# A state-space mixer on one core: convolution kernels stored in eight shifted copies, each Toeplitz block read by one 128-partition transfer

## The chip, the cores and the metric

The program runs on one core of a Trainium2 chip. TensorE (PE) multiplies, VectorE (DVE), ScalarE (ACT) and GpSimd (POOL) work elementwise, and SyncE (SP) issues transfers. ACT issues transfers too, in line with its own instructions. The metric is the device time of one execution in microseconds; the number quoted is the median of the runs.

## The reference

Sixteen meta tokens and 512 frames of width 1024, 528 positions in all, go through two layers. Layer 0 mixes along time with a diagonal state-space model; layer 1 is a windowed attention. Each layer ends with a gated feed-forward block with a short causal convolution. What matters here is the mixer of layer 0, which works on 64 groups of 16 channels, each with 64 complex states:

```python
bu = jnp.einsum('blgh,gph->blgp', ug, b_bar)
_, states = lax.associative_scan(_ssm_combine, (a, bu), axis=1)
y = jnp.einsum('blgp,ghp->blgh', states, c).real.reshape(bsz, seq_len, D_MODEL)
y = y + d_skip.astype(f32) * u32
g = jax.nn.gelu(y).astype(u.dtype)
val, gate = jnp.split(g @ w_glu, 2, axis=-1)
return val * jax.nn.sigmoid(gate)
```

## The kernel before

The mixer cuts the 528 positions into 66 chunks of T = 8 steps. Inside a chunk the recurrence is a block Toeplitz matrix (one 128 by 128 matrix for each group: 8 steps of 16 channels in, 8 steps of 16 channels out). Between chunks a scan carries the state. The 64 groups go in eight blocks of eight.

For block `b` the steps are these:

- `in_map(b)` on DVE (block 7: `input_maps` on POOL) builds the map from inputs to states, `win_t`, from powers of lambda (`own[0]`, in PSUM) and `bbar`. `input_map(b)` on PE transposes it, and on ACT it copies it to `win`.
- The normalized input `xn` is written by ACT at L783, eight instructions, one for each time step. `inputs(b)` on PE transposes it group by group, and `input_copy` on ACT copies it to `u5`, whose 128 rows are (time step, channel).
- `kernels(b)` on PE makes the convolution kernel of lags 0 to 7, and ACT copies it (L722) behind 112 columns of zeros into `kern`, 240 columns wide; the rows are (group, channel in).
- `kernel_out(b)` on ACT's queue stores those 240 columns to DRAM (`kern_scratch`).
- `kernel_in(b)` on SP's queue waits for that store and reads the Toeplitz block back into `toep` with `kernel_rows`: for each input time step t the window of 128 columns that starts at (7 - t)*16, to the 16 partitions of that step, so eight transfers for a block.
- `additions(b)` on PE and `states(b)` on DVE make the chunk states. `outputs(b)`, on PE, adds the Toeplitz product (L1179) and the states' part (L1185). Its results are called y0 to y7 below.
- `gelu(b)` on ACT evicts y, `gelu_out(b)` stores it to DRAM, and `gelu_in(b)` reads it back in eight transfers (four issued by SP, four by ACT) with channels on partitions. `glu_operand(b)` splits it for the following product `w_glu` (the GLU, L1266).

Each engine's order is written out by hand. y6 and y7 use the same two PSUM banks, so `outputs(7)` may begin only when `gelu(6)` has evicted y6; it also waits for `toep_in[7]` and for `states(7)` (`z_ready`). `toep` holds four blocks, so `kernel_in(7)` waits for y3. SP's order in this stretch is: `gelu_in(b - 4)`, then `kernel_in(b)`, for b from 4 to 7. On ACT, `kernels(b)` waits for the store of block b - 2, since `kern` has two buffers.

After the mixer PE runs the GLU, the feed-forward blocks and the attention, nearly all of it at one line, L1266.

Of the kernel before, what the change touches and what calls it, by code (L numbers as in the profile page):

```python
# [27 lines left out]
F32 = mybir.dt.float32  # L28
F32R = mybir.dt.float32r
I32 = mybir.dt.int32  # L30
ACT = mybir.ActivationFunctionType
# [3 lines left out]
P = 128  # L35
D = 1024
SEQ = 512
META = 16
L = SEQ + META
# [7 lines left out]
T = 8  # L47
# [94 lines left out]
def trunk(nc, x, meta, s5_norm, s5_lambda_re, s5_lambda_im, s5_log_step, s5_b_re, s5_b_im, s5_c_re, s5_c_im,  # L142
# [90 lines left out]
    ltmp = [at(f"ltmp{n}", Z_ZST + 512 * n, 512) for n in range(2)]  # L233
    junk = at("junk", Z_B, 2 * D)
    Z_TOEP = Z_B + G * NC + 2 * PAIRS * (T + 1) * HC
    xn = at("xn", Z_TOEP, G * TH)[:].rearrange("p (g t h) -> p g t h", g=G, t=T)
    xt_meta = at("xt_meta", Z_B + G * NC + PAIRS * (T + 1) * HC, D)

    zc = Zone(Z_C, C_COLS)
# [29 lines left out]

    zh = Zone(Z_H, KD * L)  # L270
    rhot = zh.put("rhot", PAIRS * NV)[:].rearrange("p (q c) -> p q c", q=PAIRS)
    win_t = at("win_t", Z_H + 4 * L, 2 * 2 * 4 * TH)[:].rearrange("p (b r q t h) -> p b r q t h", b=2, r=2, q=4, t=T)

    gy = x_raw.rearrange("p k (n x c) -> p k n x c", n=4, x=2)
    zh = Zone(Z_H, KD * L)
# [8 lines left out]
    same = at("same", pads(Z_SPL)[0] + 2 * TH - HC, HC)  # L284
    skip = at("skip", pads(Z_RAW)[0], KD * HC)[:].rearrange("p (k h) -> p k h", k=KD)

    kern_scratch = nc.dram_tensor("kern_scratch", (8, 8, HC, 2 * TH - HC), F32, kind="Internal").ap()
    gelu_scratch = nc.dram_tensor("gelu_scratch", (8, P, 8, NC), F32, kind="Internal").ap()

    craw = [at(f"craw{r}", Z_SPL + W_AT[r] * P, KD * S)[:].rearrange("p (e s) -> p e s", e=KD) for r in range(2)]  # L290
# [52 lines left out]
    with ctx:  # L343
# [104 lines left out]
        def bank_gone(eng, name):  # L448
# [5 lines left out]
            else:  # L454
                eng.wait_ge(gy_ready, n + 1)

        def kernel_rows(eng, b):

            for t in range(T):
                src = kern_scratch[b].rearrange("g h c -> h g c")  # L460
                eng.dma_start(toep[t * HC:(t + 1) * HC, 8 * (b % 4):8 * (b % 4 + 1), :],  # L461
                              src[:, :, (T - 1 - t) * HC:(2 * T - 1 - t) * HC]).then_inc(toep_in[b], 16)

        def gelu_rows(eng, k, groups):

# [164 lines left out]
        def _(act):  # L630
# [26 lines left out]

            def kernel_out(b):
                act.wait_ge(kern_ready, b + 1)
                act.dma_start(kern_scratch[b].rearrange("g h c -> (g h) c"), kern[b % 2][:, :]  # L660
                              ).then_inc(kern_out[b % 2], 16)

            act.dma_start(g5row[0:2, :].rearrange("p (q h) -> p q h", h=HC),
                          s5_norm[0].rearrange("(q t h) -> t q h", t=2, h=HC)).then_inc(g5_in, 16)
# [115 lines left out]
            conv_rows()  # L780
            act.wait_ge(rst5_ready, 1)
            for t in range(T):
                run(xn[0:NC, :, t, :], xc[0:NC, t * D:(t + 1) * D].rearrange("c (g h) -> c g h", g=G), ACT.Copy,  # L783
                    scale=rst5[0:NC, t:t + 1]).then_inc(xn_ready, 1)
            act.wait_ge(xn_ready, T)
            input_map(0)
# [282 lines left out]
        def _(pe):  # L1069
# [43 lines left out]
            def inputs(b):  # L1113
                if b == 0:
                    pe.wait_ge(xn_ready, T)

                    pe.wait_ge(bbar_ready, 1)
                pe.wait_ge(first_copied, U_COPIED + b - 2 if b >= 2 else C_COPIED)
                for n in range(8):
                    ins = tr(slot[b % 2][:, n // 4, (n % 4) * NC:(n % 4 + 1) * NC],  # L1120
                             xn[0:NC, 8 * b + n].rearrange("c t h -> c (t h)"), ident[0:NC, 0:NC])
                ins.then_inc(first_full, 1)

            def input_map(b):

                pe.wait_ge(*((win_dve, b + 1) if b < POOL_MAPS else (win_pool, b + 1 - POOL_MAPS)))
                if b == 0:
                    pe.wait_ge(first_copied, CONV_COPIED)
                for r in range(2):
                    ps = begin_bank(f"w{b}{'ab'[r]}")  # L1130
                    for q in range(4):
                        ins = tr(ps[:, q * P:(q + 1) * P], win_t[:, b % 2, r, q].rearrange("p t h -> p (t h)"),
                                 ident[:, :])
                    ins.then_inc(bank_full, 1)

# [31 lines left out]

            def outputs(k):

                pe.wait_ge(toep_in[k], 16 * T)  # L1170
                pe.wait_ge(z_ready, k + 1)
                ps = [begin_bank(f"y{k}{x}") for x in "ab"]

                for n in range(4):
                    o = lambda x, rows: ps[x][rows, n * NC:(n + 1) * NC]
                    for x in range(2):
                        g = 8 * k + 2 * n + x
                        for rows in (slice(0, S), slice(S, P)):
# [406 lines left out]
        def _(dve):  # L1585
# [124 lines left out]
            def in_map(b):  # L1710

                if b >= 2:
                    bank_wait(dve, f"w{b - 2}b")
                lp = [own[0][:, r * T * PAIRS:(r + 1) * T * PAIRS].rearrange("p (k q) -> p k q", k=T)
                      [:, T - 1::-1, 4 * b:4 * b + 4].rearrange("p t q -> p q t")[:, :, :, None]
                      .to_broadcast([P, 4, T, HC]) for r in range(2)]
                bb = [bbar[r][:, 4 * b:4 * b + 4, None, :].to_broadcast([P, 4, T, HC]) for r in range(2)]
                tmp = own[1].rearrange("p (q t h) -> p q t h", q=4, t=T)
                o = [win_t[:, b % 2, r] for r in range(2)]
                tt(o[0], lp[0], bb[0], ALU.mult)  # L1720
                tt(o[1], lp[0], bb[1], ALU.mult)
                link(tt(tmp, lp[1], bb[1], ALU.mult))
                link(tt(o[0], o[0], tmp, ALU.subtract))
                link(tt(tmp, lp[1], bb[0], ALU.mult))  # L1724
                tt(o[1], o[1], tmp, ALU.add).then_inc(win_dve, 1)
                dve.wait_ge(win_dve, b + 1)
# [260 lines left out]
        def _(pool):  # L1987
# [50 lines left out]
            def input_maps(b):  # L2038

                bank_wait(pool, f"w{b - 2}b")  # L2040
                lp = [lpow[r][:, T - 1::-1, 4 * b:4 * b + 4].rearrange("p t q -> p q t")[:, :, :, None]
                      .to_broadcast([P, 4, T, HC]) for r in range(2)]
                bb = [bbar[r][:, 4 * b:4 * b + 4, None, :].to_broadcast([P, 4, T, HC]) for r in range(2)]
                o = [win_t[:, b % 2, r] for r in range(2)]
                tmp = ptmp[:, :].rearrange("p (q t h) -> p q t h", q=4, t=T)
                tt(o[0], lp[0], bb[0], ALU.mult)
                link(tt(tmp, lp[1], bb[1], ALU.mult))
                tt(o[1], lp[0], bb[1], ALU.mult)
                link(tt(o[0], o[0], tmp, ALU.subtract))
                link(tt(tmp, lp[1], bb[0], ALU.mult))  # L2050
                tt(o[1], o[1], tmp, ALU.add).then_inc(win_pool, 1)
                pool.wait_ge(win_pool, b + 1 - POOL_MAPS)
# [182 lines left out]
```

## Time and profile before

| | |
|---|---|
| runs | 1170.57, 1170.91, 1167.56 us; median 1170.57 |
| profiled execution, first to last instruction (span) | 1166.7 us |
| PE busy | 1111.7 us (95% of the span) |
| DVE, ACT, POOL busy | 501.5, 484.8, 628.7 us |
| `toep` transfers | 64 of 64 KB, median 2.9 us from issue to landing |
| `kern_scratch` stores | 8 of 120 KB, median 2.8 us to landing |
| `gelu_scratch` stores | 8 of 264 KB, median 3.1 us to landing |

The page gives the profiled execution's span and no separate total; the span lies 0.9 us below the fastest run and 3.9 us below the median. The chain of waits follows the last instruction back through what released it, so its pieces add up to the span. A timeline row gives the start, the duration, the engine, the line, and in brackets how long the engine had been idle and what ended that. Rows of SPq and ACTq are those queues' issues of transfers, not the transfers themselves.

### The profile page before, as it was taken

To read this page: it belongs to the slowest core of one execution; us is meant where nothing else is said; L and a number is where in the kernel's file an instruction comes from. 1 tells how busy PE (TensorE), PEld (TensorE's weight loads), DVE (VectorE), ACT (ScalarE), POOL (GpSimd) and SP (SyncE) were. 2 spreads that over 40 slices of the span, in tenths; PEclk is the share of its full clock that TensorE was granted. 3 is DMA by queue.
4 is the path that set the end of the run, shared out by engine and by line. 5 is a ranking of instruction groups with operands and counts; after the bars stand their busy time and mean duration, and the time that the engine had idled before them with its cause. 6 is when DMAs were issued, how large, how long until landed. Compare 5 with 4: busy or idle time off the path is not lost.

```text
span 1166.7 us, 27411 instructions
## 1 busy us (share of the span) xinstructions
PE 1111.7 (95%) x10092; PEld 1070.7 (92%) x10092; DVE 501.5 (43%) x862; ACT 484.8 (42%) x885; POOL 628.7 (54%) x533
## 2 busy tenths in 40 slices
PE   4577999999999999999999999999999999999997
PEld 3466999999999999999999999999999999988887
DVE  8898312354444444211115777435444444430111
ACT  4843333354444444322324545445444444432222
POOL 4991255455555555654544454765555555565551
PEclk7598899999999999999999999999999999999999
DMA  7168432233333333333323333323333333333321
GB/s 153 31 180 177 96 94 86 74 104 88 88 88 89 89 90 94 108 92 88 96 63 84 94 102 83 88 76 102 93 93 91 90 90 90 99 110 92 95 73 73
DMA packets 221973, 110.50 MB, mean 95 GB/s; under 512 B 33271, under 2 KB 219527, under 8 KB 221591
## 3 DMA queue, kind: packets, MB, share of 16 engines
q1 hardware_dynamic: 214823, 105.41, 33.0%
q10 hardware_dynamic: 7090, 4.26, 1.4%
q8 instruction: 41, 0.67, 0.2%
q14 instruction: 19, 0.16, 0.0%
HBM read 103.31 MB, written 6.32 MB: 94 GB/s over the span
## 4 chain that ended last, share of the span: by engine, by line
PE 91%; DVE 5%; ACT 2%; issue 1%; DMA 0%; SPq 0%; POOL 0%; ACTq 0%; DVEq 0%
PE slot L1266 81%; PE slot L1547 1%; PE slot L1411 1%; PE slot L1185 1%; PE slot L1179 1%; PE slot L1462 1%; ACT xn L783 1%; PE slot L1463 1%; PE slot L1441 1%; PE slot L1148 1%; PE slot L1204 0%; DMA toep<-kern_scratch 0%; SPq L461 0%; PE slot L1524 0%; DVE slot L1724 0%
## 5 line engine op out<-in xcount | busy, mean ns | idle before, releaser
L2065 POOL TENSOR_TENSOR w_lo<-raw,w_hi 128x512 fp32r<-128x512 f32 (+2 forms) x312 | 430.6, 1383 | 428.0 <-ACT w_hi L638 409.9
L638 ACT ACTIVATE w_hi<-raw 128x512 fp32r<-128x512 f32 (+2 forms) x308 | 202.9, 662 | 394.8 <-PE slot L1266 384.5
L1266 PE MATMUL slot<-xa_hi,w_hi 128*128 128x264 f32 (+1 forms) x1472 | 298.7, 284 | 0.9 <-DVE xa_lo L1808 0.9
L1266 PE MATMUL slot<-xa_hi,w_lo 128*128 128x264 f32 (+1 forms) x1472 | 298.5, 284 | 0.0
L1266 PE MATMUL slot<-xa_lo,w_hi 128*128 128x264 f32 (+1 forms) x1472 | 298.3, 284 | 0.0
L1266 PEld LDWEIGHTS slot<-xa_hi,w_hi 128*128 128x128 f32 x1472 | 229.0, 189 | 1.3 <-issue 1.1
L1266 PEld LDWEIGHTS slot<-xa_lo,w_hi 128*128 128x128 f32 x1472 | 228.3, 189 | 0.0
L1266 PEld LDWEIGHTS slot<-xa_hi,w_lo 128*128 128x128 f32 x1472 | 227.8, 189 | 0.0
L1837 DVE TENSOR_TENSOR slot<-slot,rinv 128x528 f32<-128x528 f32 (+1 forms) x88 | 62.5, 710 | 166.8 <-PE slot L1266 166.5
L1266 PE MATMUL slot<-act_hi,w_hi 128*128 128x264 f32 (+1 forms) x506 | 132.1, 318 | 0.0
L1266 PE MATMUL slot<-act_hi,w_lo 128*128 128x264 f32 (+1 forms) x506 | 132.0, 317 | 0.0
L1266 PE MATMUL slot<-act_lo,w_hi 128*128 128x264 f32 (+1 forms) x506 | 131.7, 317 | 0.0
L1783 DVE TENSOR_TENSOR h<-slot,h 128x528 f32 (+5 forms) x23 | 16.1, 698 | 205.6 <-PE slot L1266 205.6
L1840 DVE SCALAR_TENSOR_TENSOR cbuf<-slot,conv_w,cbuf 128x528 f32<-128x528 f32 (+1 forms) x88 | 66.8, 759 | 86.3 <-ACT cbuf L900 86.3
L1266 PEld LDWEIGHTS slot<-act_lo,w_hi 128*128 128x128 f32 x506 | 83.4, 188 | 6.6
L1266 PEld LDWEIGHTS slot<-act_hi,w_lo 128*128 128x128 f32 x506 | 83.2, 188 | 6.6
L1266 PEld LDWEIGHTS slot<-act_hi,w_hi 128*128 128x128 f32 x506 | 83.4, 188 | 6.3
L1842 DVE SCALAR_TENSOR_TENSOR cbuf<-slot,conv_w,cbuf 128x528 f32<-128x528 f32 (+1 forms) x88 | 66.8, 759 | 11.5 <-DVE cbuf L1840 1.7
L900 ACT ACTIVATE cbuf<-slot,conv_w 128x528 f32<-128x528 f32 (+1 forms) x88 | 61.1, 694 | 22.7 <-DVE slot L1837 22.3
L2112 POOL TENSOR_TENSOR act_lo<-abuf,act_hi 128x528 f32 (+3 forms) x44 | 57.7, 1312 | 17.3 <-ACT act_hi L909 17.3
L905 ACT ACTIVATE slot<-cbuf 128x528 f32<-128x528 f32 (+1 forms) x44 | 26.8, 609 | 77.3 <-DVE cbuf L1842 77.3
L1266 PE MATMUL slot<-xg_hi,w_hi 128*128 128x264 f32 x256 | 53.4, 290 | 0.0
(298 smaller groups left out, 1542.9 us busy)
## 6 DMA issues: line engine op xcount, KB each, us to landing
raw<-in_ffn_w_up SPq DMA_DIRECT2D x176, 256.0 KB, 2.9
raw<-in_ffn_w_down SPq DMA_DIRECT2D x32, 384.0 KB, 3.4
raw<-in_ffn_w_down SPq DMA_DIRECT2D x32, 320.0 KB, 3.0
raw<-in_s_w_glu SPq DMA_DIRECT2D x32, 256.0 KB, 2.8
toep<-kern_scratch SPq DMA_DIRECT2D x64, 64.0 KB, 2.9
raw<-in_w_q SPq DMA_DIRECT2D x16, 256.0 KB, 3.2
raw<-in_w_o SPq DMA_DIRECT2D x16, 256.0 KB, 3.0
gelu_scratch<-x_raw ACTq DMA_DIRECT2D x8, 264.0 KB, 3.1
```

The costliest lines, as they stand in the source:

```text
L638: run(buffer_of(w_hi_all, buf, nk), buffer_of(raw_all, buf, nk), ACT.Copy).then_inc(hi_done, 1)
L783: run(xn[0:NC, :, t, :], xc[0:NC, t * D:(t + 1) * D].rearrange("c (g h) -> c g h", g=G), ACT.Copy, scale=rst5[0:NC, t:t + 1]).then_inc(xn_ ...
L900: run(cbuf[:, q, real:L], ubuf_of(q)[:, 2 + real:L + 2], ACT.Copy, scale=w).then_inc(tap_done[p], 1)
L905: run(ubuf_of(0)[:, 2 + real:L + 2], cbuf[:, 0, real:L], ACT.Silu).then_inc(silu_done[p], 1)
L1148: ins = mm(flat(b % 2)[t * S:(t + 1) * S, col:col + NV], win[b][:, r, q, t * S:(t + 1) * S], u5[:, 2 * (4 * b + q) + t, 0:NV], start=True, ...
L1266: ins = mm(slot[dst][:, half, 0:b - a], w, xx[:, k, a:b], start=k == 0 and n == 0, stop=k == nk - 1 and n == 2)
L1783: tt(hm, product(e), hm, ALU.add).then_inc(h_done[p], 1)
L1837: tt(halves(ubuf_of(q)[:, 2 + live:L + 2]), (acc_of, live_of)[l](q), halves(rinv[:, live:L]), ALU.mult).then_inc(up_evicted[p], 1)
L1840: link(stt(cbuf[:, q, real:L], ubuf_of(q)[:, 1 + real:L + 1], w(q, 1), cbuf[:, q, real:L], ALU.mult, ALU.add))
L1842: ins = stt(cbuf[:, q, real:L], ubuf_of(q)[:, real:L], w(q, 0), cbuf[:, q, real:L], ALU.mult, ALU.add)
L2065: tt(buffer_of(w_lo_all, buf, nk), buffer_of(raw_all, buf, nk), f32(buffer_of(w_hi_all, buf, nk)), ALU.subtract).then_inc(lo_done, 1)
L2112: tt(tile_of(act_lo, m, real), abuf[:, real:L], f32(tile_of(act_hi, m, real)), ALU.subtract).then_inc(act_lo_done[p], 1)
```

## The change

`kern_scratch` now holds for each block and each (group, channel in) row eight windows of 128 columns, shifted by 16 columns each, instead of the 240 columns once: the store writes 512 KB in rows of 512 bytes, from overlapping parts of `kern`, not 120 KB in rows of 960 bytes. `toep` is then read by one transfer on 128 partitions, 512 KB, not by eight on 16 partitions of 64 KB. The rows of `toep` are now ordered (channel, reversed time step), not (time step, channel). `u5`, and before it `xn` and `win_t`, have the same order: ACT writes `xn` at every eighth column, and `in_map` and `input_maps` run through time in the innermost place and through the channel outside it, with the powers of lambda in rising order.

```diff
-    xn = at("xn", Z_TOEP, G * TH)[:].rearrange("p (g t h) -> p g t h", g=G, t=T)
+    xn = at("xn", Z_TOEP, G * TH)[:].rearrange("p (g h t) -> p g h t", g=G, t=T)
...
-    kern_scratch = nc.dram_tensor("kern_scratch", (8, 8, HC, 2 * TH - HC), F32, kind="Internal").ap()
+    kern_scratch = nc.dram_tensor("kern_scratch", (8, P, T, TH), F32, kind="Internal").ap()
...
+        def windows(t):
+
+            a = t[:, 0:TH]
+            return bass.AP(tensor=a.tensor, offset=a.offset, ap=[a.ap[0], [HC, T], [1, TH]])
+
         def kernel_rows(eng, b):
 
-            for t in range(T):
-                src = kern_scratch[b].rearrange("g h c -> h g c")
-                eng.dma_start(toep[t * HC:(t + 1) * HC, 8 * (b % 4):8 * (b % 4 + 1), :],
-                              src[:, :, (T - 1 - t) * HC:(2 * T - 1 - t) * HC]).then_inc(toep_in[b], 16)
+            eng.dma_start(toep[:, 8 * (b % 4):8 * (b % 4 + 1), :],
+                          kern_scratch[b].rearrange("(g h) t c -> (h t) g c", h=HC)).then_inc(toep_in[b], 16)
...
-                act.dma_start(kern_scratch[b].rearrange("g h c -> (g h) c"), kern[b % 2][:, :]
-                              ).then_inc(kern_out[b % 2], 16)
+                act.dma_start(kern_scratch[b], windows(kern[b % 2])).then_inc(kern_out[b % 2], 16)
...
-                run(xn[0:NC, :, t, :], xc[0:NC, t * D:(t + 1) * D].rearrange("c (g h) -> c g h", g=G), ACT.Copy,
+                run(xn[0:NC, :, :, T - 1 - t], xc[0:NC, t * D:(t + 1) * D].rearrange("c (g h) -> c g h", g=G), ACT.Copy,
...
-                pe.wait_ge(toep_in[k], 16 * T)
+                pe.wait_ge(toep_in[k], 16)
...
-                      [:, T - 1::-1, 4 * b:4 * b + 4].rearrange("p t q -> p q t")[:, :, :, None]
-                      .to_broadcast([P, 4, T, HC]) for r in range(2)]
-                bb = [bbar[r][:, 4 * b:4 * b + 4, None, :].to_broadcast([P, 4, T, HC]) for r in range(2)]
+                      [:, :, 4 * b:4 * b + 4].rearrange("p t q -> p q t")[:, :, None, :]
+                      .to_broadcast([P, 4, HC, T]) for r in range(2)]
+                bb = [bbar[r][:, 4 * b:4 * b + 4, :, None].to_broadcast([P, 4, HC, T]) for r in range(2)]
```

SP's queue from `kernel_in(0)` to `gelu_in(4)`, before (`toep` is the Toeplitz block, `xt` the input for the residual stream, `x_raw` the GELU result read back):

```order
L461 DMA toep<-kern_scratch 16x8x128 x8
L522 DMA xt<-in_x 128x4x128 x8
L461 DMA toep<-kern_scratch 16x8x128 x24
L467 DMA x_raw<-gelu_scratch 16x8x66 x4
L461 DMA toep<-kern_scratch 16x8x128 x8
L467 DMA x_raw<-gelu_scratch 16x8x66 x4
L461 DMA toep<-kern_scratch 16x8x128 x8
L467 DMA x_raw<-gelu_scratch 16x8x66 x4
L461 DMA toep<-kern_scratch 16x8x128 x8
L467 DMA x_raw<-gelu_scratch 16x8x66 x4
L461 DMA toep<-kern_scratch 16x8x128 x8
L538 DMA xt_meta<-in_meta 16x1024
```

The same place with the change:

```order
L464 DMA toep<-kern_scratch 128x8x128
L525 DMA xt<-in_x 128x4x128 x8
L464 DMA toep<-kern_scratch 128x8x128 x3
L470 DMA x_raw<-gelu_scratch 16x8x66 x4
L464 DMA toep<-kern_scratch 128x8x128
L470 DMA x_raw<-gelu_scratch 16x8x66 x4
L464 DMA toep<-kern_scratch 128x8x128
L470 DMA x_raw<-gelu_scratch 16x8x66 x4
L464 DMA toep<-kern_scratch 128x8x128
L470 DMA x_raw<-gelu_scratch 16x8x66 x4
L464 DMA toep<-kern_scratch 128x8x128
L541 DMA xt_meta<-in_meta 16x1024
```

Each block has one issue in the place of eight; the sequence of steps is the same. On ACT the order stays as it was, and only the store's form differs; its rows of the change around the stores of blocks 1 to 3 are:

```order
L724 ACTIVATE kern_135<-slot 128x128
L663 DMA kern_scratch<-kern_135 1024x1x128
L715 ACTIVATE win_73<-slot 128x512 x2
L724 ACTIVATE kern_134<-slot 128x128
L663 DMA kern_scratch<-kern_134 1024x1x128
L715 ACTIVATE win_74<-slot 128x512 x2
L724 ACTIVATE kern_135<-slot 128x128
L663 DMA kern_scratch<-kern_135 1024x1x128
L752 ACTIVATE rhot<-rho 128x24x64
```

Before, those stores read `kern_scratch<-kern 128x240`; nothing else moved.

## Rows read from the trace of the kernel before

**Rows 1.** Chain of waits around y7: start us, length us, what.
```profile
109.44 3.97 DMA toep<-kern_scratch
...
113.46 0.71 PE slot L1179 x8
...
118.68 9.42 PE slot L1266 x60
```

**Rows 2.** Timeline of PE: y5 first and last, y6 first, y7 first.
```profile
102.14 0.45 PE L1179 MATMUL slot<-u,toep 128*64 128x66 f32 x8
...
104.86 0.46 PE L1185 MATMUL slot<-zst,cpow 64*64 64x66 f32 x16
107.80 0.45 PE L1179 MATMUL slot<-u,toep 128*64 128x66 f32 x8 [2.48 <-DMA toep<-kern_scratch]
...
113.46 0.71 PE L1179 MATMUL slot<-u,toep 128*64 128x66 f32 x8 [1.37 <-DMA toep<-kern_scratch]
```

**Rows 3.** Timeline of SP's queue: the eight issues of block 7.
```profile
105.23 4.65 SPq L461 DMA_DIRECT2D toep<-kern_scratch  x8
```

**Rows 4.** Timeline of DVE: the last instruction of states(0) and of states(7).
```profile
70.18 0.70 DVE L1753 TENSOR_TENSOR zst<-zprod,slot 128x520 f32<-128x520 f32 x1
...
109.30 0.70 DVE L1753 TENSOR_TENSOR zst<-zprod,slot 128x520 f32<-128x520 f32 x1
```

**Rows 5.** Timeline of ACT: kernel 3 evicted, store of block 7, gelu(5).
```profile
67.71 0.28 ACT L722 ACTIVATE kern<-slot 128x128 f32<-128x128 f32 x1 [0.48 <-PE slot L1165]
...
97.72 0.37 ACTq L660 DMA_DIRECT2D kern_scratch<-kern  x1
...
105.48 0.61 ACT L756 ACTIVATE x_raw<-slot 128x528 f32<-128x528 f32 x1 [0.36 <-PE slot L1185]
```

**Rows 6.** Windows: stretch, busy of five engines, then PEclk, DMA share, GB/s.
```profile
113.40:118.60 5.20, 5.14 (x96) 4.16 (x96) 0.71 (x1) 0.64 (x1) 0.00 (x0) 0.50 1.07 232
118.60:122.70 4.10, 4.10 (x22) 4.09 (x19) 0.15 (x1) 1.26 (x2) 0.00 (x0) 0.50 1.08 236
122.70:128.00 5.30, 5.30 (x44) 5.18 (x42) 1.27 (x2) 0.65 (x1) 0.00 (x0) 0.99 0.31 56
```

**Rows 7.** Timeline of PE: a shorter idle time earlier in the mixer.
```profile
65.44 1.09 PE L1132 MATMUL slot<-ident,win_t 128*128 128x128 f32 x8 [1.54 <-DVE win_t L1725]
```

**Rows 8.** DMA from 48 to 56 us (queue: packets, MB, share; then issues).
```profile
q1 hardware_dynamic: 1138, 0.52, 29.0%
q10 hardware_dynamic: 144, 0.12, 4.5%
...
toep<-kern_scratch SPq DMA_DIRECT2D x8, 64.0 KB, 2.4
kern_scratch<-kern ACTq DMA_DIRECT2D x1, 120.0 KB, 1.7
```

**Rows 9.** DMA from 77 to 113 us, the same view.
```profile
q1 hardware_dynamic: 8297, 3.23, 51.2%
q10 hardware_dynamic: 4320, 2.79, 29.9%
```

**Rows 10.** Groups by line on ACT: count, busy us, mean ns, idle before.
```profile
L783 ACT ACTIVATE xn<-xc,rst 66x1024 f32<-66x1024 f32 x8 | 8.4, 1135 | 1.6 <-DVE rst L1700 1.6
```

**Rows 11.** Groups by line on DVE, the same columns.
```profile
L1815 DVE TENSOR_TENSOR h<-h,sig 128x528 f32 x6 | 7.0, 1160 | 0.9 <-DVE sig L1813 0.5
...
L1813 DVE TENSOR_TENSOR sig<-slot,sig 128x528 f32<-128x528 f32 x8 | 5.7, 708 | 63.8 <-ACT sig L871 63.8
...
L1697 DVE TENSOR_TENSOR bbar<-cg,slot 128x512 f32<-128x512 f32 x1 | 0.7, 681 | 0.0
...
L1630 DVE MEMSET lpow<- 128x32 f32 x2 | 0.1, 85 | 0.1
...
L1673 DVE MEMSET phase<- 128x32 f32 x1 | 0.1, 85 | 0.0
```

**Rows 12.** Timeline of POOL: the end of its part in the mixer.
```profile
85.51 1.28 POOL L2035 TENSOR_TENSOR cpow<-cpow,ptmp 128x512 f32<-128x512 f32 x1
```

More of the change, by code:

```diff
@@ L271, in trunk @@
     rhot = zh.put("rhot", PAIRS * NV)[:].rearrange("p (q c) -> p q c", q=PAIRS)
-    win_t = at("win_t", Z_H + 4 * L, 2 * 2 * 4 * TH)[:].rearrange("p (b r q t h) -> p b r q t h", b=2, r=2, q=4, t=T)
+    win_t = at("win_t", Z_H + 4 * L, 2 * 2 * 4 * TH)[:].rearrange("p (b r q h t) -> p b r q h t", b=2, r=2, q=4, t=T)
     gy = x_raw.rearrange("p k (n x c) -> p k n x c", n=4, x=2)
@@ L1120, in inputs @@
                     ins = tr(slot[b % 2][:, n // 4, (n % 4) * NC:(n % 4 + 1) * NC],
-                             xn[0:NC, 8 * b + n].rearrange("c t h -> c (t h)"), ident[0:NC, 0:NC])
+                             xn[0:NC, 8 * b + n].rearrange("c h t -> c (h t)"), ident[0:NC, 0:NC])
                 ins.then_inc(first_full, 1)
@@ L1131, in input_map @@
                     for q in range(4):
-                        ins = tr(ps[:, q * P:(q + 1) * P], win_t[:, b % 2, r, q].rearrange("p t h -> p (t h)"),
+                        ins = tr(ps[:, q * P:(q + 1) * P], win_t[:, b % 2, r, q].rearrange("p h t -> p (h t)"),
                                  ident[:, :])
@@ L1714, in in_map @@
                 lp = [own[0][:, r * T * PAIRS:(r + 1) * T * PAIRS].rearrange("p (k q) -> p k q", k=T)
-                      [:, T - 1::-1, 4 * b:4 * b + 4].rearrange("p t q -> p q t")[:, :, :, None]
-                      .to_broadcast([P, 4, T, HC]) for r in range(2)]
-                bb = [bbar[r][:, 4 * b:4 * b + 4, None, :].to_broadcast([P, 4, T, HC]) for r in range(2)]
-                tmp = own[1].rearrange("p (q t h) -> p q t h", q=4, t=T)
+                      [:, :, 4 * b:4 * b + 4].rearrange("p t q -> p q t")[:, :, None, :]
+                      .to_broadcast([P, 4, HC, T]) for r in range(2)]
+                bb = [bbar[r][:, 4 * b:4 * b + 4, :, None].to_broadcast([P, 4, HC, T]) for r in range(2)]
+                tmp = own[1].rearrange("p (q h t) -> p q h t", q=4, t=T)
                 o = [win_t[:, b % 2, r] for r in range(2)]
@@ L2040, in input_maps @@
                 bank_wait(pool, f"w{b - 2}b")
-                lp = [lpow[r][:, T - 1::-1, 4 * b:4 * b + 4].rearrange("p t q -> p q t")[:, :, :, None]
-                      .to_broadcast([P, 4, T, HC]) for r in range(2)]
-                bb = [bbar[r][:, 4 * b:4 * b + 4, None, :].to_broadcast([P, 4, T, HC]) for r in range(2)]
+                lp = [lpow[r][:, 0:T, 4 * b:4 * b + 4].rearrange("p t q -> p q t")[:, :, None, :]
+                      .to_broadcast([P, 4, HC, T]) for r in range(2)]
+                bb = [bbar[r][:, 4 * b:4 * b + 4, :, None].to_broadcast([P, 4, HC, T]) for r in range(2)]
                 o = [win_t[:, b % 2, r] for r in range(2)]
-                tmp = ptmp[:, :].rearrange("p (q t h) -> p q t h", q=4, t=T)
+                tmp = ptmp[:, :].rearrange("p (q h t) -> p q h t", q=4, t=T)
                 tt(o[0], lp[0], bb[0], ALU.mult)
```

## The prediction

> **What bounds the kernel now.** The page's busy times (the table above) come first: PE works 1111.7 of 1166.7 us, so a change off PE pays only where PE stands still or runs slowly. The chain of waits tells where that is near the change. Most of the mixer hangs on DVE and PE in turn; at its end the transfer of the last Toeplitz block stands alone for 3.97 us, then come y7 and the GLU [rows 1]. PE's timeline shows the same transfer twice: y6 starts 2.48 us late, y7 1.37 us late, both released by `toep` [rows 2]. It was late because SP needed 4.65 us for eight issues from 105.23 on, and only the last one's landing counts [rows 3, 1], though the store it reads had been issued at 97.72 [rows 5].
>
> The windows show what these waits cost beyond themselves. PE's granted clock is 0.50, the 1.2 GHz level, in y7 and in the first 4.1 us of the GLU, and 0.99, the 2.4 GHz level, after that [rows 6]. y7 takes 118.68 - 113.46 = 5.22 us [rows 1]; y5, at full clock, takes 102.14 to 105.32, 3.18 us [rows 2].
>
> **The change, part by part.**
>
> *Issues on SP.* One issue takes the place of eight. At 4.65/8 = 0.58 us each [rows 3] seven fewer save 4.1 us on SP for every block. A block read whole has no late last part: it counts from its only issue.
>
> *The read.* Alone on the queues, 1138 packets (nearly all 512-byte rows of `toep`) took 29.0% of 16 engines over 8 us: 37.1 us, or 32.6 ns each [rows 8]. A block is 1024 such rows in either form, 1024 x 32.6 / 16 = 2.1 us of all engines. An eighth of it, 0.26 us, lands after 2.4 us [rows 8], so 2.1 us are fixed; the whole lands after about 4.2 us alone. Between 77 and 113 us the two queues keep the engines 81% busy [rows 9], so I take 5 us (ends: 4.2, and double that).
>
> *The store.* It had 128 rows; queue 10's 144 packets of 960 bytes took 4.5%, 5.8 us, 40 ns each [rows 8], or 0.3 us of all engines, and it landed after 1.7 us. Now 1024 rows at 32.6 ns are 2.1 us: 1.8 us more, so about 3.5 us alone; in traffic I take 5. The four stores in the stretch add 7.1 us to its 29.2 us of transfers (81% of 36 us) [rows 9]. This is the change's own cost, and it lies in the same queues that it relieves. Its issue on ACT took 0.37 us [rows 5]; SP's 0.58 bounds it from above, and 0.2 us once on the path (store 6) is all that adds.
>
> *When y6 and y7 can start.* Block 7: store issued at 97.72, landed at 102.7, read issued at once (SP's wait for y3 is then over), landed at about 108.3. Block 6 is a step of the mixer earlier and easily in time. So neither transfer ends the wait, and what is late next does. y6 needs the banks of y5: gelu(5) runs 105.48 to 106.09 [rows 5], and with 0.2 us to hand over (0.16 from y5's end to gelu(5)) y6 starts at 106.3 and, at 3.18 us, ends at 109.5. gelu(6) then takes 0.2 + 0.61 us, to 110.3. states(7) ends at 110.0 [rows 4]. So y7 starts at 110.5 and not at 113.46: **3.0 us** gained.
>
> *The clock.* PE would stand still for 1.0 us twice, in the place of 2.48 and 1.37 us. Earlier it stood still for 1.54 us and went on at full rate, eight transposes in 1.09 us [rows 7]. I take it that the clock stays up: y7 in 3.18, not 5.22 us, **2.0 us**; the GLU's first 4.10 us at 0.50 in 4.10 x 0.50 / 0.99 = 2.07 us [rows 6], **2.0 us**. The GLU's later operands hang on gelu(7), which moves with y7.
>
> *`xn`.* ACT writes it in eight instructions on the path, 8.4 us [rows 10]. They now write every eighth column, 32 bytes apart. No row shows ACT doing that. The ends: DVE's memset of 32 columns at far distances takes 85 ns, like the one on adjacent columns [rows 11], so nothing; and DVE's sum with one operand read at a stride takes 1160 ns where the product without takes 708 [rows 11], 0.45 us for 528 elements, 0.86 ns each, so 8 x 1024 x 0.86 = 7.0 us. I take nothing, since the memset is the row of a strided write, but it is too short to be sure.
>
> The Trainium skill, SBUF — State Buffer (section Door 1: the DMA port swizzle), says that SBUF has 16-byte lines and that each access that crosses to a new line pays a penalty, without its size. By that every element of the new `xn` write would pay; the sum would then hold the 7.0 us above and come to about zero. The strided read agrees with it; the memset does not.
>
> *`in_map`.* Only the powers of lambda are now read at a stride, 128 bytes apart in PSUM. The product at L1697 reads PSUM in just that way and takes 681 ns for 512 elements, no more than 708 for 528 without [rows 11]: nothing. On POOL block 7's four products read strided SBUF; if each took double (1.1 us more), POOL would end 4.4 us later than 86.8 [rows 12], at 91.2, still 6.5 us before the store of block 7, whose kernel needs it [rows 5]. PE's transposes and products read whole rows as before: nothing.
>
> *ACT's wait for stores.* Kernel 3 may be evicted only when the store of block 1 has landed; at 67.71 it had waited for PE alone [rows 5]. That store falls into the input's transfers, and its 1.8 us more of work (double it for the traffic) may push the eviction by up to 3.6 us. y0 and its banks wait for states(0), which end at 70.9 [rows 4], 2.9 us after the eviction, and for PE's additions behind them: covered, but for 0.7 us at the worst.
>
> **Sum**: 3.0 + 2.0 + 2.0 = 7.0 us. On the profiled span 1166.7 becomes 1159.7. That span lies 3.9 us below the median of the runs, and I set the 7.0 against the median: 1170.57 - 7.0 = **1163.6 us**. About 0.3%, 3.5 us, can be told from no change.
>
> **Rivals.**
>
> *Crowded transfers, or the clock stays down.* If stores and reads, with 7.1 us more of traffic in the same queues, land late by some 2 to 3 us, y7 starts near 112, and the long wait keeps the clock low: 1.5 us gained. If y7 starts at 110.5 but the clock falls as it did, 3.0 us. With the clock back half way, 4 to 5. For it: queues at 81%. Against it: 2.2 us of slack before y7. Together 1166 to 1169, say 1167.3.
>
> *`xn` at the strided price.* +7.0 - 7.0: **1170.5**, no change. Were the clock gain missed too, 1174.5. By itself this makes the kernel slower than before from 0.86 ns for an element on (7.0 us over 8192), and measurably from 1.28 ns: a write at a third of the rate (8.4 us become 25) would give 1180. For it: the strided read; against it: the memset. It shows in one row.
>
> *The change does not do what it says.* The single read could land as late as the last of the eight did, at 113.4 (109.44 + 3.97) [rows 1], if the engines were saturated. Then y7 stays at 113.4: 1170.6. The 4.2 us worked out above speaks against it.
>
> **How the numbers follow.** Chances: forecast 0.45; crowded transfers or low clock 0.22; strided `xn` 0.25 (of which slower than measurable 0.12); no effect, or the stores hold ACT up, 0.08. The predicted time is the likeliest, 1163.6. That case with the runs' own scatter spans 1161.5 to 1165.5; the range reaches over the second case and the even end of the third, **1161.5 to 1174**, and leaves out the steep `xn` cases above and a larger gain below. Faster by more than 0.3%: 0.45 + half of the second, 0.11 = 0.56. Slower: 0.12 + 0.03 = 0.15. The rest, 0.29, is no change.
>
> **What would show it.** Eight `toep` issues, landing 4 to 6 us; stores landing 3.5 to 6; y6 and y7 released by ACT or DVE, no longer by `toep`; granted clock 0.9 or more in y7 and the GLU's start; the eight `xn` instructions at 8.4 us. The forecast is wrong if `xn` takes 12 us or more, if `toep` still stands in the chain before y7, or if the clock is 0.50 there still.

## The result and the profile after: slower by half a per cent

The changed kernel took 1174.80 us (median of 5 runs, 1171.25 to 1175.53), beside 1168.70 us for the kernel before (5 runs, 1166.86 to 1170.91). The ratio is 1.0048, 95% interval 1.0034 to 1.0063: **5.6 us slower** (0.0048 x 1168.70), between 4.0 and 7.4. The forecast was 1163.6, and 1174.80 lies 0.8 us above its range. The forecast took its 7.0 us off 1170.57, the median of the first three of these five runs; by all five the kernel before stands 1.9 us lower. The profiled execution has a span of 1172.8 us, 6.1 more than before.

First the groups by line on ACT, the answer to [rows 10] (busy us, mean ns of one, idle before):

```profile
L785 ACT ACTIVATE xn<-xc,rst 66x1024 f32<-66x1024 f32 x8 | 15.5, 2128 | 1.1 <-DVE rst L1702 1.1
```

Eight instructions take 15.5 us where they took 8.4: **7.1 us more**, all on the path. The timelines of PE and DVE show who waits (start us, length us, engine, line, operation, and in brackets the idle time before and what ended it):

```profile
47.24 2.02 PE L1122 MATMUL slot<-ident,xn 66*128 66x66 f32 x16 [7.32 <-ACT xn L785]
```
```profile
55.71 0.69 DVE L1722 TENSOR_TENSOR win_t<-slot,bbar 128x512 f32<-128x512 f32 x1 [9.61 <-PE slot L1134]
...
116.00 0.70 DVE L1755 TENSOR_TENSOR zst<-zprod,slot 128x520 f32<-128x520 f32 x1
```

PE stands still for 7.32 us for `xn`, and DVE stands still for 9.61 us because of that. The last instruction of states(7) starts at 116.00, 6.7 us later than before (109.30 [rows 4]). That delay never shrinks on the way: the last instruction of states(0) comes at 76.89, 6.7 us later too (70.18 [rows 4]), and y7, which ACT releases in the end, starts 6.8 us later (120.24, before 113.46 [rows 2]).

Then the transfers, from 77 to 113 us as in [rows 9] (queue: packets, MB, share; then issues: KB each, median us to landing):

```profile
q10 hardware_dynamic: 7639, 4.36, 40.2%
q1 hardware_dynamic: 8123, 3.47, 36.4%
...
toep<-kern_scratch SPq DMA_DIRECT2D x5, 512.0 KB, 4.5
kern_scratch<-kern ACTq DMA_DIRECT2D x4, 512.0 KB, 6.1
```

One issue for a block, landing after 4.5 us, and stores landing after 6.1: much as forecast (5 and 5). The share of ACT's queue went from 29.9 to 40.2%. PE's timeline is the answer to [rows 2]:

```profile
96.86 0.45 PE L1150 MATMUL slot<-u,win 128*64 128x65 f32 x6 [1.36 <-issue]
...
110.89 0.45 PE L1181 MATMUL slot<-u,toep 128*64 128x66 f32 x8 [0.77 <-ACT x_raw L758]
...
115.30 0.46 PE L1181 MATMUL slot<-u,toep 128*64 128x66 f32 x8 [1.02 <-ACT x_raw L758]
...
120.24 0.45 PE L1181 MATMUL slot<-u,toep 128*64 128x66 f32 x8 [1.62 <-ACT x_raw L758]
```

`toep` releases nothing any more, so this part of the change does what it says. In its place stand waits for ACT's GELU before y5, y6 and y7, and a standstill of 1.36 us in the middle of the additions before y3, ended by nothing that the profile shows ("issue"). ACT's timeline shows why it is late for the GELU:

```profile
91.14 0.52 ACTq L663 DMA_DIRECT2D kern_scratch<-kern  x1
91.70 4.21 ACTq L470 DMA_DIRECT2D x_raw<-gelu_scratch  x4
...
115.51 3.24 ACTq L470 DMA_DIRECT2D x_raw<-gelu_scratch  x4
118.85 0.64 ACT L766 ACTIVATE xg_hi<-x_raw 128x528 fp32r<-128x528 f32 x1 [3.80 <-issue]
119.40 0.59 ACT L758 ACTIVATE x_raw<-slot 128x528 f32<-128x528 f32 x1
```

The four issues that read GELU rows back take 4.21 us behind a store of 1024 rows, and gelu(6), at 119.40, stands in the same instruction stream behind four such issues and an operand copy. Last the windows, as [rows 6] (the column before the last two is the granted clock):

```profile
118.00:122.00 4.00, 2.38 (x72) 1.97 (x70) 0.72 (x2) 1.14 (x2) 0.00 (x0) 0.97 0.98 237
122.00:128.00 6.00, 6.00 (x64) 5.50 (x63) 0.71 (x1) 1.63 (x3) 0.00 (x0) 0.50 0.96 225
```

PE is at the 2.4 GHz level (granted clock 0.97) until 122 and at 1.2 GHz (0.50) for the rest of y7 and the GLU's start. y7 takes 124.44 - 120.24 = 4.20 us in place of 5.22, and that 1.0 us is all the clock gave.

### The profile page after: what moved, and what is told of

Read it like the earlier page. It is cut to its first block, busy times and chain, and to the rows that moved or that the text cites. A ratio compares the mean times of both kernels' runs of the same rounds, so it can differ in the third digit from the quotient of the medians.

```text
span 1172.8 us, 27355 instructions
## 1 busy us (share of the span) xinstructions
PE 1109.1 (95%) x10092; PEld 1068.6 (91%) x10092; DVE 500.9 (43%) x862; ACT 491.8 (42%) x885; POOL 629.7 (54%) x533
## 4 chain that ended last, share of the span: by engine, by line
PE 90%; DVE 5%; ACT 3%; issue 1%; DMA 1%; ACTq 1%; SPq 0%; DVEq 0%
PE slot L1268 81%; PE slot L1549 1%; ACT xn L785 1%; PE slot L1413 1%; PE slot L1464 1%; PE slot L1187 1%; PE slot L1181 1%; PE slot L1465 1%; PE slot L1443 1%; ACTq L470 1%; PE slot L1150 0%; PE slot L1206 0%; DMA v_scratch<-vtok 0%; PE slot L1526 0%; DVE slot L1726 0%
```

## The experiments

Three parts had to be told apart: the strided write of `xn`, the larger store, and the single read. Each of the first runs undoes some of them or does some of them alone; later ones change the order of the issues or the engine that writes. Times are ratios to the kernel before on the same chip, with the 95% interval; us are the ratio's difference from 1 times some 1169 us.

**The change with `xn` in runs of 16.**
```diff
-    xn = ... .rearrange("p (g h t) -> p g h t", g=G, t=T)
+    xn = ... .rearrange("p (g t h) -> p g t h", g=G, t=T)
-                run(xn[0:NC, :, :, T - 1 - t], ...
+                run(xn[0:NC, :, T - 1 - t, :], ...
```


> Leaves out the right order of the rows of xn: the changed kernel, but ACT writes xn in runs of 16 channels of one time step again and the transposes take the rows as they lie, so the values fed to the mixer are in another order than the powers expect. All else as in the changed kernel: stores in eight copies, one read for a block, POOL's and DVE's products at a stride. Theory A (the strided write of xn costs 7.1 us on the path, and what the single read gains is eaten afterwards by ACT): the eight xn instructions fall to about 8.4 us, the inputs' transposes start near 40.5 us, y7 starts near 113 and the time is 1 to 2 us under the kernel before, ratio 0.998 to 1.000. Theory B (the forecast was right but for xn): y7 starts at 110.5, the clock stays up, and the time is 7 us under the kernel before, ratio 0.994. Theory C (the stores and their traffic cost as much as xn does): 2 to 4 us over the kernel before, ratio 1.002 to 1.003.

Measured: 1167.15 us, ratio 0.9992 (0.9974 to 1.0009): within theory A's range, 0.9 us under the kernel before, which the interval does not tell from none. `xn` is back at 8.4 us (1135 ns each). Theory B, that all else of the forecast holds, fell: y7 starts at 113.40, where the kernel before had it at 113.46 [rows 2], and not at 110.5. Theory C's 1.002 to 1.003 did not come either.

```profile
90.62 0.45 PE L1150 MATMUL slot<-u,win 128*64 128x65 f32 x6 [1.36 <-issue]
...
104.55 0.45 PE L1181 MATMUL slot<-u,toep 128*64 128x66 f32 x8 [0.67 <-ACT x_raw L758]
...
108.75 0.45 PE L1181 MATMUL slot<-u,toep 128*64 128x66 f32 x8 [1.02 <-ACT x_raw L758]
...
113.40 0.45 PE L1181 MATMUL slot<-u,toep 128*64 128x66 f32 x8 [1.46 <-ACT x_raw L758]
```

These are PE's rows of that run: y5 starts 2.4 us later than the 102.14 of [rows 2], mostly by the standstill and the wait for gelu(4), and y7 2.9 us later than forecast.

**The kernel before with the strided `xn`.**
```diff
-                run(xn[0:NC, :, t, :], xc[0:NC, ...
+                run(xn[0:NC, :, :, t], xc[0:NC, ...
```


> Leaves out the right order of the rows of xn: the kernel before, with the one edit that ACT writes xn 32 bytes apart and the transposes take the rows as they lie. Stores and reads of Toeplitz blocks as before. Theory A (the strided write alone is on the path in full): the eight xn instructions take 15.5 us in place of 8.4, and the time is 6.5 to 7.5 us over the kernel before, ratio 1.0055 to 1.0065. If the waits for toep before y6 and y7 took part of it up (the transfers have more time while DVE is late), 2 to 4 us, ratio 1.002 to 1.0035.

Measured: 1175.70 us, ratio 1.0059 (1.0046 to 1.0072): **6.9 us slower** for this one edit, theory A. Its group on ACT:

```profile
L783 ACT ACTIVATE xn<-xc,rst 66x1024 f32<-66x1024 f32 x8 | 15.5, 2124 | 0.2 <-DVE rst L1700 0.2
```

The late transfers took none of it up. The wait before y6 fell to 1.02 us, but that before y7 grew to 3.86, since block 7's issues come when SP gets to them, and SP's steps moved with everything else.

**The store alone**, still with eight reads.
```diff
-                act.dma_start(kern_scratch[b].rearrange("g h c -> (g h) c"), kern[b % 2][:, :]
+                act.dma_start(kern_scratch[b], windows(kern[b % 2])
...
-                src = kern_scratch[b].rearrange("g h c -> h g c")
+                src = kern_scratch[b].rearrange("(g h) t c -> t h g c", h=HC)
...
```


> The kernel before, with its blocks stored in eight shifted copies of 128 columns (1024 rows of 512 bytes in place of 128 of 960), and read by the same eight transfers of 16 partitions. xn as before. Theory A (the larger store delays what the queues carry, and ACT's own issues behind it): the store lands after 5 to 6 us in place of 2 to 3, block 7's read is issued 1 to 2 us later or not at all later, ACT's issues of the gelu rows take longer than the 1.9 us for four that they took, and the time is 1 to 3 us over the kernel before, ratio 1.001 to 1.0025. Rival (the store is hidden whole): ratio 1.000 within 0.001, and ACT's issues for four rows stay near 2 us; then it is the whole reads and not the stores that slow ACT's issues in the changed kernel.

Measured: 1172.79 us, ratio 1.0030 (1.0018 to 1.0042): **3.5 us slower**, theory A, and a little above its upper end. PE's timeline:

```profile
96.80 0.35 PE L1190 MATMUL slot<-zst,cpow 64*64 64x66 f32 x9 [1.58 <-issue]
...
111.32 0.71 PE L1184 MATMUL slot<-u,toep 128*64 128x66 f32 x8 [3.97 <-DMA toep<-kern_scratch]
...
117.56 0.71 PE L1184 MATMUL slot<-u,toep 128*64 128x66 f32 x8 [1.02 <-ACT x_raw L761]
```

y6 waits 3.97 us for its block (before: 2.48), y7 starts at 117.56, 4.1 us later, and the standstill is here too, without any single read.

**All GELU issues of the first seven steps on SP**, on top of the first run.
```diff
-                gelu_rows(sp, k, range(SP_ROWS))
+                gelu_rows(sp, k, range(8 if k < 7 else SP_ROWS))
...
+                if k < 7:
+                    return
```


> Leaves out the right order of the rows of xn, as the run with xn in runs of 16 does, and moves one thing more: SP issues all eight transfers that read the gelu rows of a step back, and ACT none, for the first seven steps. Theory A (ACT's issues of the gelu rows stand in front of its evictions and so hold up y6 and y7): y6 and y7 start 1 to 2 us earlier than in that run, no wait of PE for ACT over 1 us is left before y5, y6 and y7, and the time is 2 to 4 us under that run. Rival (ACT is late for its evictions for another reason, or SP's issues then make the transfers late): no more than 0.5 us apart, or slower.

Measured: 1169.81 us, ratio 1.0000 (0.9986 to 1.0014), 0.9 us above the first run by the ratios: the rival. The waits did fall as theory A said, to nothing before y5 and 1.02 before y7, 1.1 us in all, but three standstills of 0.34, 1.64 and 0.70 us ("issue") made up for it, and y7 starts at 113.58. ACT's issues do delay the GELU, but taking them off ACT gains nothing while standstills take its place.

**The single read alone**, with the old small store.
```diff
...
+            src = bass.AP(tensor=a.tensor, offset=a.offset,
+                          ap=[[HC - 1, P], [HC * (2 * TH - HC), 8], [1, TH]])
+            eng.dma_start(toep[:, 8 * (b % 4):8 * (b % 4 + 1), :], src).then_inc(toep_in[b], 16)
```


> Leaves out the right Toeplitz blocks: the kernel before, with the old small store (128 rows of 960 bytes) and xn as it was, but each block read by one transfer of 128 partitions, each row of which starts 60 bytes after the last and so is not the row that the mixer wants. It is the single read without the larger store and without the strided xn. Theory D (the larger store takes the forecast gain: its traffic holds up PE's instructions, 1.36 us within the additions before y3 and 0.5 us before y2, and ACT's issues of the gelu rows, 1.1 us before y5 and y7): without it y2 to y5 start as in the kernel before (y5 at 102.1 to 102.6), y6 near 106.4, y7 near 110.6, and the profiled span is near 1160 if the clock stays up, the median 4 to 7 us under the kernel before, ratio 0.994 to 0.9965. Rival (the whole reads themselves slow ACT and PE): y7 near 113 as in the run with xn in runs of 16, ratio 0.998 to 1.000.

Measured: 1163.79 us, ratio 0.9955 (0.9942 to 0.9968): **5.3 us faster**, theory D. This is the part of the change that the forecast was about, and its size:

```profile
89.62 0.45 PE L1148 MATMUL slot<-u,win 128*64 128x65 f32 x6 [0.52 <-issue]
...
106.84 0.45 PE L1179 MATMUL slot<-u,toep 128*64 128x66 f32 x8 [1.02 <-ACT x_raw L756]
...
111.60 0.45 PE L1179 MATMUL slot<-u,toep 128*64 128x66 f32 x8 [1.18 <-ACT x_raw L756]
```

y6 starts at 106.84 (forecast 106.3) and y7 at 111.60 (110.5). ACT's four issues ahead of gelu(6), in the kernel before and then in this run:

```profile
106.50 2.04 ACTq L467 DMA_DIRECT2D x_raw<-gelu_scratch  x4
```
```profile
107.01 3.09 ACTq L467 DMA_DIRECT2D x_raw<-gelu_scratch  x4
```

This run measures a part and is no kernel to keep.

**The change's store and read, nothing else of it.**
```diff
+                act.dma_start(kern_scratch[b], windows(kern[b % 2])
...
+            eng.dma_start(toep[:, 8 * (b % 4):8 * (b % 4 + 1), :],
+                          kern_scratch[b].rearrange("(g h) t c -> (h t) g c", h=HC)).then_inc(toep_in[b], 16)
```


> Leaves out the right order of the Toeplitz rows: the kernel before with the change's store (eight copies, 1024 rows of 512 bytes) and its single read in the order channel, time step, but with xn and the input maps in the old order, so that they do not match. It is the change without any strided write or product. Theory D (the larger store alone takes back what the single read gains): like the run with xn in runs of 16, PE stands still over 1 us within the additions or products before y3, y7 starts near 113, ratio 0.998 to 1.000. Rival (the difference between that run and the run with the single read alone came from the strided products on POOL and DVE): like the single read alone, y7 near 111, ratio 0.9955.

Measured: 1168.19 us, ratio 0.9998 (0.9986 to 1.0011): theory D. The strided products on DVE and POOL are not in this run, and it does as the first run did (0.9992), so they cost nothing that can be told. Against the single read alone, the eight larger stores cost 0.9998 - 0.9955 = 0.0043, **5.0 us** (some 3 to 7 by the two intervals). y7 starts at 113.45:

```profile
90.61 0.45 PE L1151 MATMUL slot<-u,win 128*64 128x65 f32 x6 [1.64 <-issue]
...
104.59 0.46 PE L1182 MATMUL slot<-u,toep 128*64 128x66 f32 x8 [0.73 <-ACT x_raw L759]
...
113.45 0.71 PE L1182 MATMUL slot<-u,toep 128*64 128x66 f32 x8 [1.48 <-ACT x_raw L759]
```

The windows of this run and of the first one show the clock's price by itself, since y7 starts within 0.05 us in both. Here (y7, then the GLU's start):

```profile
113.40:118.60 5.20, 5.15 (x97) 4.19 (x97) 0.75 (x2) 0.64 (x1) 0.00 (x0) 0.50 1.08 250
118.60:122.00 3.40, 3.40 (x26) 3.40 (x23) 0.00 (x0) 0.76 (x2) 0.00 (x0) 0.78 0.54 135
```

and in the first run:

```profile
113.40:116.50 3.10, 3.10 (x96) 2.56 (x96) 0.14 (x1) 0.64 (x1) 0.00 (x0) 1.00 1.09 253
116.50:122.00 5.50, 5.50 (x52) 5.49 (x46) 1.28 (x2) 1.26 (x2) 0.00 (x0) 1.00 0.77 190
```

At 1.2 GHz y7 takes 5.2 us, at 2.4 GHz 3.1; the spans are 1165.9 and 1163.1. In the slower one the clock comes back early in the GLU: a mean of 0.78 over 3.4 us leaves an estimated 1.5 us at 1.2 GHz there (3.4 x 0.22 / 0.50). PE's waits before y6 and y7 are the same in both, 1.02 and 1.48 here, 1.02 and 1.46 there.

**One of the eight stores small, and one large.** The block is number 5, whose store and read precede y3.
```diff
-                act.dma_start(kern_scratch[b], windows(kern[b % 2])
+                act.dma_start(*((kern_small..., kern[b % 2][:, :]) if b == 5
+                                else (kern_scratch[b], windows(kern[b % 2])))
```


> Leaves out the right Toeplitz rows, as the run with the change's store and read alone does; and block 5 alone is stored small (128 rows of 960 bytes) and read with rows that start 60 bytes apart. Seven larger stores are left. In the run with all eight, block 5's store was issued at 84.6, the store's queue kept the engines busy to 105% from 88 to 89, ACT's four issues of gelu rows at 85.2 took 3.1 us and PE stood still for 1.64 us within the additions before y3. Theory D1 (block 5's larger store makes both): the stand-still falls to 0.3 to 0.6 us, the four issues to 1.9 to 2.0, and y3 starts at 92.8 to 93.1 in place of 94.04; y7 1 us earlier, near 112.4; the ratio is too small a change to tell from the run with all eight, 0.997 to 0.9995. Rival (the stand-still is a matter of the reads, or of the order of instructions): 1.3 us or more is left.

> The reverse: seven blocks stored small, and block 5 alone in eight copies; values left out in the same way. Theory D1: PE stands still for 1.3 to 1.7 us before y3 and the four issues of ACT at 85 take 3 us or more, as with all eight large; y5 and y7 lose little more to ACT, since the stores of blocks 6 and 7 are small, so y7 starts near 112.3, between 111.6 and 113.45. Rival: a stand-still of 0.3 to 0.6 us as in the run with the single read alone (0.52).

Measured: 1167.68 us with block 5 alone small, ratio 0.9988 (0.9972 to 1.0004); 1165.02 us with block 5 alone large, 0.9969 (0.9953 to 0.9985). ACT's four issues behind block 5's store, first with it small, then large:

```profile
88.36 1.97 ACTq L475 DMA_DIRECT2D x_raw<-gelu_scratch  x4
```
```profile
86.55 3.28 ACTq L475 DMA_DIRECT2D x_raw<-gelu_scratch  x4
```

Both as theory D1 said: the larger store ahead in ACT's queue slows the issues behind it. The standstill is another matter. PE's rows, again small and then large:

```profile
93.99 0.45 PE L1157 MATMUL slot<-u,win 128*64 128x65 f32 x6 [1.64 <-issue]
```
```profile
97.64 0.35 PE L1194 MATMUL slot<-zst,cpow 64*64 64x66 f32 x9 [1.03 <-issue]
```

With block 5 small the 1.64 us stay where they were, against D1 (and 1.14 more stand within y0, so that run's steps are all later); with it alone large, 1.03 us come at a later place, within y3. So no single store makes that standstill.

**SP's order in place of the change.** In the kernel before, block 7 was issued from 105.23 on [rows 3], behind GELU rows that nobody needed yet. This edit leaves store, read and `xn` alone.
```diff
             for b in range(4, 8):
-                gelu_in(b - 4)
                 bank_wait(sp, f"y{b - 4}b")
                 kernel_in(b)
+                gelu_in(b - 4)
```


> The kernel before, with two calls of SP's queue in another order: the eight issues that read Toeplitz block b come ahead of the four that read gelu rows of step b - 4, for b from 4 to 7. Store, reads and xn as before. If what made block 7 late was its place in SP's queue (issued from 105.23 on, behind the gelu rows at 103.21, when its store of 97.72 had landed near 100), its issues begin near 101, its last part lands near 109, y6 and y7 wait for ACT alone (1.02 us), y7 starts at 110.5 to 111, and the median is 4 to 7 us under the kernel before, ratio 0.994 to 0.9965; 3 us, 0.9975, if the clock falls all the same. Rival (the gelu rows come late instead and hold up the GLU's operands, or the eight issues simply wait for the store): ratio 0.999 to 1.001.

Measured: 1167.10 us, ratio 0.9989 (0.9980 to 0.9998): 1.3 us faster, between the two. y6 no longer waits for its block, but block 7 is issued at 103.36 and not near 101, since the rows of step 2 still stand ahead of it, and y7 starts at 112.55 after 4.02 us of waiting:

```profile
103.36 4.72 SPq L461 DMA_DIRECT2D toep<-kern_scratch  x8
```

So the next two take blocks 6 and 7 ahead of those rows too; the first of them also copies each step into the GLU's operand one step later on ACT.
```diff
...
+            bank_wait(sp, "y2b")
+            kernel_in(6)
+            bank_wait(sp, "y3b")
+            kernel_in(7)
+            gelu_in(2)
+            gelu_in(3)
...
-                if b >= 3:
-                    glu_operand(b - 3)
+                if b >= 4:
+                    glu_operand(b - 4)
```


> The kernel before with SP's queue in a third order: blocks 6 and 7 of the Toeplitz rows ahead of the gelu rows of steps 2 and 3, and ACT's copy of a gelu step into the GLU's operand one step later (with a semaphore for each step), so that ACT does not wait for those rows ahead of gelu(6). In the first reordering block 7 was issued from 103.36 on, behind the gelu rows of step 2 (101.34), and y7 still waited 4.02 us for it and started at 112.55. Theory E (only the place in SP's queue is left): block 7 is issued from 101.3 on, y7 waits for ACT or for toep by no more than 2 us and starts at 110.5 to 111, ratio 0.9945 to 0.997. Rival (eight transfers in the traffic take so long that the place does not matter, or the GLU then waits for its operands): ratio 0.998 to 1.000.

> The same order of SP's queue, but ACT's copies of the gelu steps left where they were. Block 7 is as early as in the run beside it, but ACT now waits for the gelu rows of step 2 ahead of gelu(6), which PE needs before y7. If that wait ends last, y7 starts at 112 to 113, and the ratio is 0.997 to 0.999; if the rows are there in time, the same as the run beside it.

Measured: 1166.36 us, **ratio 0.9975 (0.9964 to 0.9986)**, 2.9 us faster, just outside theory E's 0.997, though y7's start is where it said. With ACT's copies left where they were, 1168.84 us, 0.9995 (0.9986 to 1.0004). PE's rows before y7, first of the one, then of the other:

```profile
110.32 0.46 PE L1187 MATMUL slot<-u,toep 128*64 128x66 f32 x8 [1.73 <-DMA toep<-kern_scratch]
```
```profile
114.40 0.71 PE L1186 MATMUL slot<-u,toep 128*64 128x66 f32 x8 [3.96 <-ACT x_raw L763]
```

In the second, ACT waits 6.00 us for the GELU rows of step 2 in front of gelu(6), and y7 waits for ACT in place of `toep`. The first beats both kernels: by the ratios it is 2.9 us under the one and 8.5 (2.9 + 5.6) under the other.

**Three of the strided writes on DVE**, in the changed kernel.
```diff
-            for t in range(T):
+            for t in range(T - 3):
                 run(xn[0:NC, :, :, T - 1 - t], ...
...
+                    for t in range(T - 3, T):
+                        ts(xn[0:NC, :, :, T - 1 - t], ..., rst5[0:NC, t:t + 1], None, ALU.mult)
```


> The changed kernel, with three of the eight strided xn writes taken from ACT and given to DVE, which writes them behind in_map(0), where it has 9.61 us of idle time. ACT's five take 9.6 us in place of 15.5; if DVE's price for a strided write is no more than ACT's (1.9 us each, 5.8 for three), xn is ready about 6 us earlier, y7 starts 5 to 6 us earlier, near 114.5, and the median is 4 to 6 us under the changed kernel's, ratio to the kernel before 0.999 to 1.001. If DVE's writes cost 3 us each or the squares and DVE's earlier work come in the way, the gain is 2 us or less, ratio 1.003.

Measured: 1170.73 us, ratio 1.0017 (1.0000 to 1.0034), 3.6 us under the changed kernel by the ratios, a little short of the 4 to 6 expected. DVE's price, in its groups by line:

```profile
L1771 DVE TENSOR_SCALAR xn<-xc,rst 66x1024 f32<-66x1024 f32 x3 | 5.0, 1769 | 0.0
```

The mean is over three unlike ones, 1227, 1974 and 2107 ns; ACT's five in this run take 2097 to 2161. The transposes start at 43.18 and not 47.24, y7 at 115.88 and not 120.24.

All of them side by side (`xn` strided or not, stores large or small, reads of a block):

| run | `xn` | stores | reads | y7 starts | ratio |
|---|---|---|---|---|---|
| kernel before | runs | small | 8 | 113.46 | 1 |
| changed kernel | strided | large | 1 | 120.24 | 1.0048 |
| `xn` in runs of 16 | runs | large | 1 | 113.40 | 0.9992 |
| the same, GELU issues on SP | runs | large | 1 | 113.58 | 1.0000 |
| store and read alone | runs | large | 1 | 113.45 | 0.9998 |
| one of eight stores small | runs | 7 large | 1 | 116.45 | 0.9988 |
| one of eight stores large | runs | 1 large | 1 | 113.03 | 0.9969 |
| read alone | runs | small | 1 | 111.60 | 0.9955 |
| before, strided `xn` | strided | small | 8 | 119.40 | 1.0059 |
| store alone | runs | large | 8 | 117.56 | 1.0030 |
| three writes on DVE | strided | large | 1 | 115.88 | 1.0017 |
| SP's order, first | runs | small | 8 | 112.55 | 0.9989 |
| SP's order, second, ACT's copies later | runs | small | 8 | 110.32 | 0.9975 |
| SP's order, second | runs | small | 8 | 114.40 | 0.9995 |

y7's start is that of one profiled execution and the ratio that of all runs, so they need not go in step: with seven stores large the profile has an early delay of its own.

## Why the prediction was wrong

**By parts.** The read alone gains 5.3 us, the larger stores cost 5.0, the strided `xn` 6.9: together 6.6 slower, and 5.6 (4.0 to 7.4) was measured.

- ***`xn`* is the step that failed.** The forecast gave nothing for it, with 7.0 as the other end, and 7.1 us of busy time and 6.9 of the whole were measured. It had taken a memset of 32 columns for the row of a strided write, and that row was too short to show a price per element. One instruction grew by 0.97 ns for an element ((2128 - 1135) / 1024), and the eight, which overlap a little, by 7.1 / 8192 = 0.87 ns; at either price 32 elements are some 30 ns, which the 85 ns of a short instruction may hide (not tried). The longer row, DVE's strided read [rows 11], gave 0.86 ns; it is another engine's price, for a read, and yet it came out right. The rival "`xn` at the strided price" had 0.25 and is the right account of `xn`. That its figure with the clock's gain missed, 1174.5, is so near to 1174.80 is in part luck: it still held the 3.0 us from the read, which the stores took back, and it was counted from 1170.57 and not from 1168.70. The Trainium skill's SBUF — State Buffer (section Door 1: the DMA port swizzle) has 16-byte lines and a penalty for each access that crosses into a new one. The trace agrees: 2128 ns in place of 1135.
- **The store, "1.8 us each" and 0.2 us on the path.** Its own landing was near (5 forecast, 6.1 measured), and so was its issue (0.52 us, bounded by 0.58). What failed is the sentence that only the issue, 0.2 us, lies on the path. The sum took y5's start, 102.14, from the kernel before, as if the steps before it stayed. In the run with store and read alone y5 starts at 104.59. In the profiles 1.85 us of y7's delay are the stores': 113.45 against 111.60 with the read alone, of which 1.12 are the standstill (1.64 against 0.52), and most of the rest is gelu(4), late before y5 (0.73 against none). The other 3 of the 5.0 us are not seen in these two profiles, and where they lie is not shown. The span of the run with the read alone, 1164.2, belongs to the longest of its five times.
- **The read.** One issue, 4.5 us to landing (5 forecast), and `toep` gone from PE's waits: right. With the read alone y6 and y7 start 0.5 and 1.1 us after the forecast.
- **"I take it that the clock stays up."** The price in y7 was right (2.0 forecast): two runs with the same starts differ by 2.1 us there. The other 2.0 us, in the GLU, were not seen at that size; the spans of the two differ by 2.8 in all. The condition failed. After waits of 1.02 and about 1.5 us PE was at 2.4 GHz in one of them and at 1.2 in the other, after 1.02 and 1.18 with the read alone its granted clock was 0.50 from 114 to 118, and in the changed kernel it fell at 122. The twelve times of the first run go roughly with their mean granted clock, from 1163.71 us at 0.978 to 1174.80 at 0.968. A gain from the clock is a chance here, and 4.0 us of it was too much to put in a sum.
- **"So neither transfer ends the wait, and what is late next does."** Right, and ACT was named. That ACT would itself be later was missed: its four issues ahead of gelu(6) take 3.09 us in place of 2.04 even with the read alone. Why is not shown: no larger store stands ahead of them there, and SP issues beside them in both.
- **`in_map` at nothing**: right. DVE's products with strided powers take 678 to 699 ns, as [rows 11] had it (681). POOL's four products with strided SBUF take 1351 to 1373 ns, beside 1105 to 1113 for the same four before; POOL ends at 87.4 (before: 86.8) and has room.
- **"ACT's wait for stores", covered**: right. With the store alone kernel 3's eviction waited 1.76 us for a store to land, with store and read alone 0.83; the last instruction of states(0) came at 69.80 and 69.86, no later than before (70.18).

The standstill of PE that ends with "issue" was, between 72 and 116 us, 1.0 us or more in each profile here with any larger store and at most 0.52 without, but with block 5's store made small it stayed. No view names a releaser, but the DMA rows hold a companion, a packet of 16 KB on a queue called "instruction", here from 88 to 89 us in the run with store and read alone:

```profile
q8 instruction: 1, 0.02, 6.9%
```

That is 1.10 us (0.069 x 16); in the trace the packet lasts from 88.11 to 89.21, and PE goes on at 90.61. In all 14 such standstills of 0.25 us or more in that stretch, over the kernel before, the changed one and the runs, PE goes on 1.25 to 1.58 us after the end of such a packet, nine times at the same instruction of its program. So PE very likely waits for its own next instructions. Why their packet comes later where stores are larger stays open.

## What to carry to other kernels

Price an element-wise instruction whose layout becomes strided from the longest strided row there is, never from a tiny one, and ask who waits behind it: here eight writes at nearly twice the time outweighed a whole transfer scheme. A transfer that is late because of its place in an issuing queue is first moved in that queue, which adds no traffic: here one line moved gained 1.3 us, and 2.9 came when the copies that need the delayed rows were moved too. And a larger store can cost more than its own landing: here the issues right behind it took longer on an engine that has evictions to make, and PE stood still, very likely for its own instructions.

## What the runs showed of the hardware that was not expected

- ACT writing f32 elements 32 bytes apart in SBUF took 2128 ns for 1024 columns, adjacent runs of 16 took 1135; DVE took 1227 to 2107 ns for the same strided write (three of them). Reading PSUM at 128 bytes cost DVE nothing (678 to 699 ns, before 680 to 699).
- Issues can cost by what stands before them. The store of 1024 rows itself took 0.52 to 0.60 us to issue, that of 128 rows 0.33 to 0.37, but the four issues right after it took 3.28 us in place of 1.97. The Trainium skill's DMA: Bandwidth & Descriptors (section Anatomy of one DMA, of GpSimd's path) says that one can emit a lot of descriptors before the incremental cost shows up. On ACT's queue here 1024 rows showed it, and in the issues behind the store more than in its own.
- PE stood still for up to 1.64 us in mid-stream and went on 1.25 to 1.58 us after a 16 KB packet of the "instruction" queue had ended, 14 times of 14.
